# mLSTM heads by row groups and column groups, four modulation tiles in each head, and one modulation part computed beside the first dense product

## The chip, the cores and the metric

The kernel runs on 1 core of a Trainium2 chip. The metric is the device time of one execution in microseconds (us), the median over runs. Everything is float32; the large products are made from float32r halves (high and low parts), the small ones directly in float32.

## The reference

One layer of a decoder trunk on 256 prompt tokens and 8 sample sequences of 4 tokens (288 columns in all, N). Cut to what the change touches:

```python
mod = silu(c) @ w_ada + b_ada            # 9 rows; w_ada is 2048 x 12288
sh_a, sc_a, g_a, sh_c, sc_c, g_c = split(mod, 6)
h = rmsnorm(x, g) * (1 + sc_a) + sh_a
z = h @ w_in                             # the first dense product
# mLSTM, for each of 4 heads, state C (128 x 256) and n (128) per sequence
S    = (q @ k.T) * exp(logD - m)
num  = S @ v + w_inter * (q @ C)         # q @ C: the past state
den  = sum(S) + w_inter * (q @ n)
h    = num / max(abs(den), exp(-m))
C_new = dC * C + (ws * k).T @ v          # the update, one for each sequence
n_new = dC * n + sum(ws * k)
h    = h * rsqrt(mean(h * h) + eps)      # then gain and sigmoid(o)
x = x + g_a * (concat(rwkv, mlstm) @ w_out)
```

## The kernel before

The program is written out by hand for each engine, with semaphores; nothing is scheduled by a planner. Its stages in order of time:

* Modulation, parts 0 and 1. A part is 2048 columns of `w_ada` and comes as 16 tiles of 1 MiB through a ring of four SBUF slots (`ring`), loaded by SyncE's queue in program order. One `ada_step` on TensorE is one tile: 16 matmuls with 32 columns of weights and 128 moving columns, four of them side by side in the four column groups of the array. Four steps fill one bank; ScalarE copies it out (`ada_take`), and after a whole part `ada_turn` turns it and ScalarE stores it (`ada_store`).
* The first dense product, 50 tiles of `w_in` through the same ring. For each tile ScalarE makes the high half (`hi`), GpSimd the low half (`lo`), and TensorE runs 48 matmuls of 288 columns (`dense`). In the first 8 tiles ScalarE also feeds a convolution on VectorE and waits for it within each tile; then 8 tiles of v, 8 of o, and 26 of the RWKV part.
* Broadcasts and transposes for the mLSTM, then its 4 heads, then the RWKV-7 stage, then `w_out`, `w_q` and 256 PEER tiles, which take the time from about 945 us on.
* The 96 tiles of modulation parts 2 to 7 are handled between about 457 us and 900 us, as filling: `ada_more(count)` stands at fixed places in TensorE's stream, and takes the next `count` steps from one list, in order.

One mLSTM head h on TensorE before: after `s_ready` (VectorE's masked scores) three products into banks 1 to 3, in which the past state enters by 16 matmuls of 4 moving columns with a fresh 128x128 weight each; then nine updates (8 sequences and the prompt) one after the other in banks 4 and 5, each waiting until VectorE has used the bank two before; the scores of the next head; the sum of squares; and 7 modulation steps spread between. VectorE makes the denominator (`rec`), `hh`, the decays of the next head, and takes each update with two instructions: the state (128x256) and the normaliser (128x1). The state of each head is loaded and stored by GpSimd's queue (1 MiB each way).

Of the kernel before, what the change touches and what calls it, by code (L numbers as in the profile page):

```python
# [30 lines left out]
P = 128  # L31
# [21 lines left out]
def columns(sizes):  # L53
# [11 lines left out]
    ("seye", SM), ("sincl", SM), ("seq", NB), ("wreset", N), ("breset", N), ("mreset", N), ("sel", BH * P), ("fold", 4 * NS), ("seqcol", NB * SM), ("comp", 38)])  # L65
# [44 lines left out]
def constants():  # L110
# [50 lines left out]
    put(c1, CST1, "fold", fold)  # L161
    put(c1, CST1, "seqcol", np.broadcast_to(np.repeat(np.eye(NB), TS, axis=1), (P, NB, SM)))
# [16 lines left out]
def build(nc, T):  # L179
    ctx = ExitStack()  # L180
    with ctx:
# [45 lines left out]
        adas = words(M_ADAS, D)  # L227
        ymix = words(M_YMIX, KT, N)
# [38 lines left out]
        ktok_s = words(q6 + 2 * BH * P, BH, P, rows=SM)  # L267
        q7 = q6 + 3 * BH * P
        vtok = words(q7, 2, BH, DV + 1)
        vtok_s = words(q7 + 2 * BH * (DV + 1), BH, DV + 1, rows=SM)  # L270
# [6 lines left out]
        kwm = words(q4, NB, P, rows=SM)  # L277
        assert NB * P <= 4 * (ZXW + 1)
# [123 lines left out]
        wg_hi, wg_lo = parts("wg_hi", za, KT, 36), parts("wg_lo", za + KT * 36, KT, 36)  # L402
# [14 lines left out]
        n_wo = n_ada1 + 6 * ADA_TILES  # L417
# [74 lines left out]
        def ada_tile(j, quarter):  # L492

            return (n_ada0 + j * KT if j < 2 else n_ada1 + (j - 2) * KT) + 4 * quarter
# [8 lines left out]
        def parts_turned(j):  # L503

            return j + 4 if j else 1

# [6 lines left out]
        def _(sp):  # L513
# [27 lines left out]

            for j in range(2):
                ada(j)
            tiles(n_z, T["w_in"], 24, AT)
            tiles(n_z + 24, T["w_in"], 24)
            for j in range(2):
                load(n_z + 48 + j, T["w_in"][24 + j])
            for j in range(2, 8):
                ada(j)
# [149 lines left out]
        def _(pe):  # L699
# [14 lines left out]
            def ada_turn(j):  # L714

                pe.wait_ge(S("ada_copied"), 4 * (j + 1))
                if j > 2:
                    pe.wait_ge(S("mods_raw"), parts_turned(j - 1))
# [4 lines left out]
            def ada_step(j, quarter, q):  # L723
# [4 lines left out]
                if q == 0 and j > 2 and quarter == 1:  # L728
                    pe.wait_ge(S("mods_raw"), parts_turned(j - 1))
# [9 lines left out]
                if quarter == 0 and j > 0 and j != 2 and q == 3:  # L739
                    ada_turn(j - 1)  # L740
# [5 lines left out]
            pending = [(j, quarter, q) for j in range(2, 8) for quarter in range(4) for q in range(4)]  # L746
# [7 lines left out]
            def dense(n, hi, lo, i, bank, split=None):  # L754

                w_hi, w_lo = hi_slot(n), ring_lo[:, n % RING_SLOTS]
                for kt in range(KT):
                    if kt % 8 == 0:
                        pe.wait_ge(S("lo_ready"), i * 8 + (2 * dense_index(n) + kt // 8 + 1))
# [20 lines left out]
            pe.wait_ge(S("cond_ready"), 1)  # L780
# [34 lines left out]
            with pe.Fori(0, 6) as i:  # L815
                for j in range(4):
                    pe.wait_ge(S("z_free"), i * 4 + (24 + j + 1))
                    dense(n_z + 24 + j, h_hi, h_lo, i, j % 2, "h")
# [17 lines left out]
            for q, name in enumerate(("g", "ws")):  # L836
                for b in range(3):
                    w = P if b < 2 else SM
                    at = 4 * (2 * b + q)
                    mm = turn(ps[1][0:w, at:at + 4], row[name][:, b * P:b * P + w])  # L840
# [5 lines left out]
            for u, (what, b, g) in enumerate(fills):  # L846
                if u >= 4:
                    pe.wait_ge(S("turn_done"), u - 3)
                w = P if b < 2 else SM
                for j in range(4):  # L850
                    src = bv[:, 4 * g + j, b * P:b * P + w] if what == "v" else qk[:, BH + j, b * P:b * P + w]
                    mm = turn(ps[u % 4][0:w, j * P:(j + 1) * P], src)
# [11 lines left out]
            scores(0)  # L864
            for h in range(BH):
                pe.wait_ge(S("s_ready"), h + 1)
                pe.wait_ge(S(f"c_landed{h % 2}"), 16 * (h // 2 + 1))
                if h:
                    pe.wait_ge(S("num_used"), h)
                for half in range(3):  # L870
                    def vt(b, rows=P):
                        if half == 2:
                            return ones[0:rows, :]
                        src = vtok[:, b, h] if b < 2 else vtok_s[:, h]
# [4 lines left out]
                    mm = matmul(out[:, TP:N], vt(2, SM), dd[0:SM, 1, TP + P:DW], True, False)  # L879
                    if half < 2:  # L880
                        for b in range(NB):
# [3 lines left out]
                    else:  # L885
                        mm = matmul(out[:, TP:N], ones, qw[:, 1, :], False, True)
                mm.then_inc(S("num_ready"), 1)

                pe.wait_ge(S("kwm_ready"), h + 1)
                if h:  # L890
                    pe.wait_ge(S("ms_root"), h)
                    pe.wait_ge(S("upd_used"), h * NS)
                for u in range(NS):
                    if u >= 2:
                        pe.wait_ge(S("upd_used"), h * NS + u - 1)
                    out = ps[4 + u % 2][:, 0:DV + 1]
                    if u < NB:
                        mm = matmul(out, kwm[:, u, :], vtok_s[:, h, :])
                    else:
                        matmul(out, ktok[:, 0, h, :], vtok[:, 0, h, :], True, False)  # L900
# [1556 lines left out]
```

## Time and profile before

| what | us |
|---|---|
| median of 3 runs | 2921.88 (2921.21 to 2929.64) |
| the profiled execution | 2921.68 |
| its span, first to last instruction | 2919.9 |
| PE busy, POOL busy, DVE busy, ACT busy | 2725.9, 1771.7, 1121.3, 951.9 |
| mean granted TensorE clock | 0.955 |

How it is read. The windows view gives for a stretch of time its length, then the busy time and the count of instructions (x) of PE, PEld (weight loads), DVE (VectorE), ACT (ScalarE) and POOL (GpSimd), the granted TensorE clock (1.00 is 2.4 GHz, 0.50 is 1.2 GHz), the mean busy share of the DMA engines, and GB/s. The timeline gives start, duration, engine, line, operation, output and inputs with shapes, the count merged into the row, and in brackets the idle time before it with what released it. One float32 matmul leaves two records, so a modulation step of 16 matmuls is 32 records. The waits view gives the total, the number of times and the longest one. DMA issues give a median time from issue to landing.

### The profile page before, as it was taken

Reading aid. Unit: us, or ns where it says so; the run is one execution under the profiler, and the core shown is the slowest. Engines: PE = TensorE matmul, PEld = TensorE weight load, DVE = VectorE, ACT = ScalarE, POOL = GpSimd, SP = SyncE. Lnnn points to the kernel's source line nnn. Section 1 sums busy time; section 2 is a strip of 40 time slices with the busy share of each in tenths; the row PEclk is TensorE's granted clock in tenths of the full one; section 3 lists DMA queues with packets and bytes.
Section 4 is the critical chain, followed back from the end, with each engine's and each line's share of the span. In section 5 each row is a group of like instructions: output and inputs, shape, how many; then the busy total and the mean of one; then the engine's idle time right before and its main releaser. Section 6 shows DMA issues by size and latency. Waiting matters only on the chain.

```text
span 2919.9 us, 62759 instructions
## 1 busy us (share of the span) xinstructions
PE 2725.9 (93%) x25899; PEld 2620.6 (90%) x25899; DVE 1121.3 (38%) x2241; ACT 951.9 (33%) x1353; POOL 1771.7 (61%) x745
## 2 busy tenths in 40 slices
PE   5789999979875989999999999999999999999997
PEld 3689997768763979899999999999999999999997
DVE  0450664464237120896477313200131101455134
ACT  1343432131112333444333333333333333332333
POOL 0267771003211677688655577777777777888775
PEclk9899997679986999999999999999999999999999
DMA  9744445888664434344455444555544555554442
GB/s 374 263 142 165 165 160 212 290 294 285 233 208 162 159 126 162 130 158 158 174 182 181 164 171 159 179 185 187 177 159 172 184 182 189 185 183 174 169 163 104
DMA packets 150467, 544.94 MB, mean 187 GB/s; under 512 B 8984, under 2 KB 18856, under 8 KB 121512
## 3 DMA queue, kind: packets, MB, share of 16 engines
q1 hardware_dynamic: 136672, 505.18, 49.0%
q10 hardware_dynamic: 11480, 20.44, 1.9%
q0 software_dynamic: 2160, 17.03, 1.5%
q8 instruction: 125, 2.05, 0.3%
q14 instruction: 30, 0.25, 0.0%
HBM read 518.77 MB, written 23.84 MB: 186 GB/s over the span
## 4 chain that ended last, share of the span: by engine, by line
issue 39%; POOL 35%; PE 21%; DVE 3%; ACT 1%; POOLq 1%; DMA 0%; DVEq 0%; ACTq 0%
POOL ring_lo L605 34%; PE bank L701 21%; PE bank L704 0%; DVE staged L2106 0%; DVE y_lo L1758 0%; DMA kept<-in_w_ada 0%; POOLq L604 0%; DVE staged L2059 0%; ACT hi_peer L1337 0%; POOLq L609 0%; DVE staged L2093 0%; POOL h_lo L675 0%; POOL staged L694 0%; DVE staged L2095 0%; POOL staged L683 0%
## 5 line engine op out<-in xcount | busy, mean ns | idle before, releaser
L605 POOL TENSOR_TENSOR ring_lo<-kept,hi_peer 128x1024 fp32r<-128x1024 f32 x576 | 1441.6, 2526 | 496.9 <-ACT hi_peer L1337 496.9
L1337 ACT ACTIVATE hi_peer<-kept 128x1024 fp32r<-128x1024 f32 x576 | 578.1, 1051 | 1134.0 <-PE bank L701 1133.9
L701 PE MATMUL bank<-h_hi,ring_lo 128*128 128x288 f32 x3104 | 914.0, 294 | 0.0
L701 PE MATMUL bank<-h_hi,hi_peer 128*128 128x288 f32 x2304 | 686.1, 298 | 18.1 <-DVE h_lo L2152 10.3
L701 PE MATMUL bank<-h_lo,hi_peer 128*128 128x288 f32 x2304 | 680.7, 295 | 0.0
L701 PE MATMUL bank<-act_hi,hi_peer 128*128 128x288 f32 x2048 | 604.8, 295 | 6.7 <-POOL ring_lo L605 3.6
L701 PE MATMUL bank<-act_hi,ring_lo 128*128 128x288 f32 x2048 | 604.5, 295 | 0.0
L701 PE MATMUL bank<-act_lo,hi_peer 128*128 128x288 f32 x2048 | 604.2, 295 | 0.0
L701 PEld LDWEIGHTS bank<-h_hi,ring_lo 128*128 128x128 f32 x3104 | 585.8, 189 | 0.0
L701 PEld LDWEIGHTS bank<-h_hi,hi_peer 128*128 128x128 f32 x2304 | 432.4, 188 | 21.4 <-issue 16.2
L701 PEld LDWEIGHTS bank<-h_lo,hi_peer 128*128 128x128 f32 x2304 | 433.3, 188 | 0.0
L701 PEld LDWEIGHTS bank<-act_hi,hi_peer 128*128 128x128 f32 x2048 | 384.8, 188 | 8.4 <-POOL ring_lo L605 8.4
L701 PE MATMUL bank<-staged 64*64 64x64 f32 (+10 forms) x5264 | 339.9, 267 | 52.6 <-issue 18.3
L701 PEld LDWEIGHTS bank<-act_hi,ring_lo 128*128 128x128 f32 x2048 | 385.1, 188 | 0.0
L701 PEld LDWEIGHTS bank<-act_lo,hi_peer 128*128 128x128 f32 x2048 | 384.9, 188 | 0.0
L701 PEld LDWEIGHTS bank<-staged 64*64 64x64 f32 (+5 forms) x5264 | 283.3, 153 | 102.4 <-issue 51.8
L605 POOL TENSOR_TENSOR ring_lo<-kept,hi_front 128x1024 fp32r<-128x1024 f32 x100 | 243.3, 2453 | 205.1 <-ACT hi_front L1337 205.1
L2273 DVE CAST act_hi<-staged 128x576 fp32r<-128x576 f32 (+1 forms) x128 | 84.9, 663 | 578.1 <-PE bank L701 578.1
L701 PE MATMUL bank<-h_hi,hi_front 128*128 128x288 f32 x800 | 236.4, 296 | 11.4 <-POOL ring_lo L605 11.4
L701 PE MATMUL bank<-h_lo,hi_front 128*128 128x288 f32 x800 | 236.7, 296 | 0.0
L701 PE MATMUL bank<-kept,staged 128*32 128x128 f32 x4144 | 176.9, 328 | 64.0 <-DMA kept<-in_w_ada 36.9
L701 PEld LDWEIGHTS bank<-kept,staged 128*32 128x32 f32 x4144 | 137.9, 132 | 98.4 <-DMA kept<-in_w_ada 44.5
(219 smaller groups left out, 2371.0 us busy)
## 6 DMA issues: line engine op xcount, KB each, us to landing
kept<-in_peer_u SPq DMA_DIRECT2D x128, 1024.0 KB, 4.7
kept<-in_peer_v SPq DMA_DIRECT2D x128, 1024.0 KB, 5.5
kept<-in_w_ada SPq DMA_DIRECT2D x96, 1024.0 KB, 8.6
kept<-in_w_in SPq DMA_DIRECT2D x50, 1024.0 KB, 4.7
kept<-in_w_adaf SPq DMA_DIRECT2D x32, 1024.0 KB, 5.6
kept<-in_w_out SPq DMA_DIRECT2D x16, 1024.0 KB, 4.8
kept<-in_w_q SPq DMA_DIRECT2D x16, 1024.0 KB, 4.7
gates_spill<-staged ACTq DMA_DIRECT2D x24, 576.0 KB, 3.0
```

What stands on the lines that cost most here:

```text
L605: pool.tensor_tensor(ring_lo[:, n % RING_SLOTS, cols], ring[n % RING_SLOTS][:, cols], hi_slot(n)[:, cols].bitcast(F32), ALU.subtract).then ...
L701: return pe.matmul(out, lhsT, rhs, start=start, stop=stop)
L1337: return act.activation(out, in_, ACT.Copy)
L2273: dve.tensor_copy(act_hi[:, n % 2], a).then_inc(S("acts_hi"), 1)
```

## The change

It has three parts.

1. In the heads, the updates of the 8 sequences are made by 32-row matmuls: the keys of the 4 sequences of a half are masked so that each 32-row group holds one sequence (`kwm`, now 2 x 128 columns over 128 partitions in place of 8 x 128 over 32), and four updates go to four banks in the four row groups. The past state is applied by `qwm` (the queries masked by sequence, 32 columns of weights) with the state as moving data, 256 columns, in the four column groups of bank 0; ScalarE copies that bank to `past`, and two small matmuls add it to banks 1 and 2. The normaliser's eight small instructions become three for all sequences, with one matmul of 8 columns. The order inside a head changes on all three engines.
2. Each head has four modulation steps in one run at its end (`ada_more(4)`), in place of seven spread out, and one more stands ahead of the first head.
3. Modulation part 2 (`G_A`, 16 tiles) is computed in the first 16 tiles of the dense product, from two SBUF buffers of its own (`early`), with loads put between those of `w_in` in SyncE's queue. The list for `ada_more` has 80 steps in place of 96.

```diff
-            pending = [(j, quarter, q) for j in range(2, 8) for quarter in range(4) for q in range(4)]
+            pending = [(j, quarter, q) for j in range(2 + EARLY_PARTS, 8) for quarter in range(4) for q in range(4)]
+
+            def early_step(i, q):
+                pe.wait_ge(S(f"early{q % 2}_landed"), i * 32 + 16 * (q // 2 + 1))
+                if q == 0:
+                    pe.wait_ge(S("ada_copied"), i + 8)
+                for k_ in range(4):
+                    for g in range(4):
+                        mm = matmul(ps[6][32 * g:32 * g + 32, 0:P], silc[:, 4 * q + k_, :],
+                                    early[q % 2][:, k_ * 512 + g * P:k_ * 512 + (g + 1) * P],
+                                    q == k_ == 0, q == k_ == 3)
+                mm.then_inc(S("early_used"), 1)
+
+            def early_turn(i):
+                pe.wait_ge(S("ada_copied"), i + 9)
+                matmul(ps[7][:, bass.ds(i * (4 * NS), 4 * NS)], early_row, cst1("fold")).then_inc(S("ada_turned"), 1)
...
-            with pe.Fori(0, 6) as i:
+            with pe.Fori(0, EARLY_BODIES) as i:
                 for j in range(4):
                     pe.wait_ge(S("z_free"), i * 4 + (j + 1))
-                    dense(n_z + j, h_hi, h_lo, i, j % 2, "h")
+                    dense(n_z + j, h_hi, h_lo, i, j % 2, "h", {0: 0, 2: 3}.get(j))
+                    if j < 2:
+                        early_step(i, j + 1)
+                early_turn(i)
...
+            def update(h, u, bank):
+                pe.wait_ge(S("upd_used"), h * NS + (u - 3 if u >= 4 else 0))
+                matmul(ps[bank][:, 0:DV], kwm[QUAD[u % 4], u // 4, :], vtok_s[QUAD[u % 4], h, 0:DV]).then_inc(S("upd_ready"), 1)
...
+                for b in range(NB):
+                    mm = matmul(ps[0][QUAD[b % 4], 0:DV], qwm[:, b, :], cring[:, h % 2, b, :], b < 4, b >= 4)
+                mm.then_inc(S("num_ready"), 1)
...
-                            mm = matmul(out[:, TP + b * TS:TP + (b + 1) * TS],
-                                        cring[:, h % 2, b, half * P:(half + 1) * P], qw[:, 0, b * TS:(b + 1) * TS],
-                                        False, b == NB - 1)
...
+                for half in range(2):
+                    mm = matmul(ps[1 + half][:, TP:N], past[:, half * P:(half + 1) * P], cst1("seye"), False, True)
...
+                for u in range(4):
+                    update(h, u, 4 + u)
+                pe.wait_ge(S("head_taken"), 2 * h + 2)
+                for i in range(2):
+                    mm = matmul(ps[3][:, 0:N], ones, hsq[:, i, :], i == 0, i == 1)
+                mm.then_inc(S("ms_ready"), 1)
+                for u in range(4, NB):
+                    update(h, u, u)
+                pe.wait_ge(S("upd_used"), h * NS + 5)
...
                 pe.wait_ge(S("upd_used"), h * NS + NS - 1)
-                ada_more(3)
+                ada_more(4)
```

What stands there on TensorE after the products of the first head, from its first update on (banks by number; `kept,staged 32x128` is a modulation step, 257 columns are a state and its normaliser). Before:

```order
L701 MATMUL bank4<-staged 128x257
L701 MATMUL bank5<-staged 128x257
L701 MATMUL bank7<-kept,staged 32x128 x32
L701 MATMUL bank4<-staged 128x257
L701 MATMUL bank5<-staged 128x257
L701 MATMUL bank4<-staged 128x257
L701 MATMUL bank7<-kept,staged 32x128 x16
L701 MATMUL bank5<-staged 128x257
L701 MATMUL bank4<-staged 128x257
L701 MATMUL bank5<-staged 128x257
L701 MATMUL bank4<-staged 128x257 x2
L701 MATMUL bank0<-staged 128x256
```

And of the change, from the last of the next head's scores on:

```order
L748 MATMUL bank0<-staged 32x32
L748 MATMUL bank4<-staged 128x256
L748 MATMUL bank5<-staged 128x256
L748 MATMUL bank6<-staged 128x256
L748 MATMUL bank7<-staged 128x256
L748 MATMUL bank3<-staged,kept 128x288 x2
L748 MATMUL bank4<-staged 128x256
L748 MATMUL bank5<-staged 128x256
L748 MATMUL bank6<-staged 128x256
L748 MATMUL bank7<-staged 128x256
L748 MATMUL bank4<-staged 128x257 x2
L748 MATMUL bank4<-staged 128x8
```

The updates stand in fours, the sum of squares (bank 3) between them, the next head's scores ahead of them, and no modulation step among them; behind the last row come 64 matmuls of modulation.

ScalarE at the end of the third and the start of the fourth tile in a body of the first dense loop (the convolution's sigmoid, then the high half of a coming tile). Before:

```order
L1337 ACTIVATE staged<-bank 128x256 [waits zq_free]
L1337 ACTIVATE staged<-bank 128x8x4
L1337 ISA
L1337 ACTIVATE staged<-staged 128x8x3
L1334 ACTIVATE staged<-staged 128x312 [waits conv_ready]
L1432 REGISTER_ALU
L1337 ACTIVATE hi_front_51<-kept 128x1024 [waits weights_used,slot1_landed]
```

And of the change:

```order
L1409 ACTIVATE staged<-staged 128x312 [waits conv_ready]
L1447 REGISTER_ALU
L1448 REGISTER_ALU [waits early_used]
L1412 ACTIVATE staged<-bank 128x128 [waits ada_turned]
L1515 REGISTER_ALU
L1412 ACTIVATE hi_front_51<-kept 128x1024 [waits weights_used,slot1_landed]
```

The copy of the modulation row (128x128) now stands between the sigmoid of one tile and the high half of the next; TensorE's `early_turn` at the end of the body waits for it.

## Rows read from the trace of the kernel before

**Rows 1.** Windows: first dense tiles, then the four heads.

```profile
135.00:200.00 65.00, 56.09 (x404) 54.45 (x402) 44.80 (x59) 27.54 (x52) 39.27 (x17) 0.97 0.38 132
488.30:522.40 34.10, 34.10 (x307) 26.46 (x307) 14.04 (x36) 3.46 (x7) 3.21 (x6) 0.60 0.45 149
522.40:555.00 32.60, 32.17 (x319) 24.51 (x315) 17.29 (x41) 5.01 (x9) 1.61 (x3) 0.69 0.89 322
555.00:587.40 32.40, 32.40 (x309) 25.00 (x306) 14.01 (x36) 4.67 (x7) 1.07 (x2) 0.63 0.78 276
587.40:620.00 32.60, 26.22 (x311) 20.27 (x311) 18.60 (x33) 1.74 (x4) 1.61 (x3) 0.79 0.89 317
```

**Rows 2.** Waits in the heads, 488 to 620 us.

```profile
DVE staged L1920 <- PE bank L701: 37.7, 4, 12.1
```

**Rows 3.** Timeline of PE in the second head.

```profile
522.38 6.43 PE L701 MATMUL bank<-staged 128*128 128x256 f32 x44
...
533.36 3.64 PE L701 MATMUL bank<-kept,staged 128*32 128x128 f32 x64
536.93 3.14 PE L701 MATMUL bank<-staged 32*128 32x257 f32 x6
...
541.87 6.62 PE L701 MATMUL bank<-staged 32*128 32x257 f32 x15
```

**Rows 4.** Timeline of PE in the RWKV stage: a modulation step at full clock.

```profile
663.22 1.08 PE L701 MATMUL bank<-kept,staged 128*32 128x128 f32 x32
664.23 1.98 PE L701 MATMUL bank<-staged 64*64 64x128 f32 x64
```

**Rows 5.** Timeline of DVE in the second head.

```profile
531.46 0.46 DVE L1920 SCALAR_TENSOR_TENSOR staged<-bank,staged 128x288 f32<-128x288 f32 x1 [7.40 <-PE bank L701]
...
535.17 0.68 DVE L1744 TENSOR_SCALAR staged<-staged 128x256 f32<-128x256 f32 x3
535.77 0.17 DVE L1899 TENSOR_TENSOR staged<-staged 128x32 f32<-128x32 f32 x1
...
536.09 0.48 DVE L1936 SCALAR_TENSOR_TENSOR staged<-staged,bank 128x256 f32<-128x256 f32 x1
536.48 0.21 DVE L1937 SCALAR_TENSOR_TENSOR staged<-staged,bank 128x1 f32<-128x1 f32 x1
...
548.60 0.27 DVE L1907 TENSOR_TENSOR staged<-staged 128x128 f32<-128x128 f32 x1
...
549.68 0.17 DVE L1912 TENSOR_TENSOR staged<-bank,staged 32x32 f32<-32x32 f32 x1
551.25 1.95 DVE L1947 RECIPROCAL staged<-staged 128x288 f32<-128x288 f32 x1 [1.40 <-ACT staged L1340]
```

**Rows 6.** Timeline of PE from the last head to the RWKV stage.

```profile
610.89 1.96 PE L701 MATMUL bank<-kept,staged 128*32 128x128 f32 x64
613.46 1.08 PE L701 MATMUL bank<-kept,staged 128*32 128x128 f32 x32 [0.62 <-DMA kept<-in_w_ada]
619.76 1.94 PE L701 MATMUL bank<-kept,staged 128*32 128x128 f32 x32 [5.22 <-DMA kept<-in_w_ada]
...
627.30 1.24 PE L701 MATMUL bank<-staged 64*128 64x288 f32 x8
```

**Rows 7.** DMA issues between 457 and 682 us.

```profile
kept<-in_w_ada SPq DMA_DIRECT2D x51, 1024.0 KB, 7.7
```

**Rows 8.** Waits from 115 to 457 us, the first dense product.

```profile
PE bank L701 <- POOL ring_lo L605: 11.4, 8, 2.7
```

**Rows 9.** Timeline of ACT: high halves of two convolution tiles, then of two later ones.

```profile
148.41 2.00 ACT L1337 ACTIVATE hi_front<-kept 128x1024 fp32r<-128x1024 f32 x2
...
156.24 1.99 ACT L1337 ACTIVATE hi_front<-kept 128x1024 fp32r<-128x1024 f32 x2
...
207.23 2.02 ACT L1337 ACTIVATE hi_front<-kept 128x1024 fp32r<-128x1024 f32 x2 [5.81 <-PE bank L701]
...
213.41 2.01 ACT L1337 ACTIVATE hi_front<-kept 128x1024 fp32r<-128x1024 f32 x2 [3.88 <-PE bank L701]
```

**Rows 10.** Timeline of PE at the start of the first head.

```profile
488.27 9.43 PE L701 MATMUL bank<-staged 128*128 128x256 f32 x44 [2.25 <-DVE staged L1912]
```

**Rows 11.** Timeline of PE late in the sample states.

```profile
878.48 2.83 PE L701 MATMUL bank<-kept,staged 128*32 128x128 f32 x96
```

More of the change, by code:

```diff
@@ L401, in build @@
         assert q5 + D + KT * N <= za
-        wg_hi, wg_lo = parts("wg_hi", za, KT, 36), parts("wg_lo", za + KT * 36, KT, 36)
+        early = [words(q5 + D + KT * N + b * D, D) for b in range(2)]
+        assert (q5 + D + KT * N) % 8 == 0 and q5 + D + KT * N + 2 * D <= za + MT * N
+        wg_at = za + MT * N
+        wg_hi, wg_lo = parts("wg_hi", wg_at, KT, 36), parts("wg_lo", wg_at + KT * 36, KT, 36)
         y_hi, y_lo = parts("y_hi", m_yhi, KT, N), parts("y_lo", M_YMIX, KT, N)
@@ L836, in _ @@
             for q, name in enumerate(("g", "ws")):
-                for b in range(3):
-                    w = P if b < 2 else SM
+                for b in range(2):
                     at = 4 * (2 * b + q)
-                    mm = turn(ps[1][0:w, at:at + 4], row[name][:, b * P:b * P + w])
+                    turn(ps[1][:, at:at + 4], row[name][:, b * P:(b + 1) * P])
+                for g in range(4):
+                    mm = matmul(ps[1][QUAD[g], 4 * (4 + q):4 * (4 + q) + 4], row[name][:, TP:N], ident[0:BH, 0:BH])
             mm.then_inc(S("cols_ready"), 1)
@@ L848, in _ @@
                     pe.wait_ge(S("turn_done"), u - 3)
[L849 removed]
                 for j in range(4):
[L851 to L852 removed]
+                    src = bv[:, 4 * g + j] if what == "v" else qk[:, BH + j]
+                    if b < 2:
+                        mm = turn(ps[u % 4][:, j * P:(j + 1) * P], src[:, b * P:(b + 1) * P])
+                        continue
+                    for c in range(4):
+                        mm = matmul(ps[u % 4][QUAD[c], j * P:(j + 1) * P], src[:, TP:N], ident)
                 mm.then_inc(S("turn_ready"), 1)
@@ L887, in _ @@
-                mm.then_inc(S("num_ready"), 1)
[L889 to L900, printed above, removed]
-                        mm = matmul(out, ktok[:, 1, h, :], vtok[:, 1, h, :], False, True)
-                    mm.then_inc(S("upd_ready"), 1)
-                    if u in (1, 4):
-                        ada_more(2 if u == 1 else 1)
+                    matmul(out[:, TP:N], vt(2, SM), dd[0:SM, 1, TP + P:DW], True, False)
@@ L909, in _ @@
+                out = ps[4][:, 0:DV + 1]
+                matmul(out, ktok[:, 0, h, :], vtok[:, 0, h, :], True, False)
+                matmul(out, ktok[:, 1, h, :], vtok[:, 1, h, :], False, True)
+                matmul(ps[4][:, DV + 1:DV + 1 + NB], ktok_s[0:SM, h, :], cst1("seq", rows=SM)).then_inc(S("upd_ready"), 1)
                 pe.wait_ge(S("upd_used"), h * NS + NS - 1)
-                for i in range(2):
-                    mm = matmul(ps[5][:, 0:N], ones, hsq[:, i, :], i == 0, i == 1)
```

204 lines of the change are left out of this document (128 added, 76 removed).

## Prediction

> **What bounds the kernel now.** I read the windows first, because the page's 93% for TensorE is a mean over stages with different limits and the change touches two of them. In the four heads TensorE is busy for nearly the whole stretch, VectorE for about half of it, and the granted clock is 0.60 to 0.79, so TensorE runs mostly at the lower of its two levels [rows 1]. The head starts stand at 488.3, 522.4, 555.0 and 587.4 us, a pitch of 99.1 / 3 = 33.0 us. The waits then say who is kept waiting: VectorE waits for TensorE at the start of its denominator, 37.7 us in four heads [rows 2], and the timeline shows TensorE going from one block to the next, updates, modulation steps and products [rows 3]. So a head is bound by the length of TensorE's stream, at a low clock. The last head is followed by a stretch in which TensorE waits for modulation tiles, 0.62 and 5.22 us [rows 6]. The first dense product is another matter. In its first 8 tiles ScalarE sets the pace: its high halves come every 156.24 - 148.41 = 7.83 us, and TensorE waits for the low halves behind them 8 times, 11.4 us in all [rows 8, 9]. Later they come at 213.41 - 207.23 = 6.18 us, which is TensorE's own pace, and whatever is added to TensorE there lengthens the stage. The PEER tiles are not touched.
>
> **Part 3, the early tiles.** Added: 16 steps and 4 turns. A step between other work at full clock takes 664.23 - 663.22 = 1.01 us [rows 4], so 16.2 us, and four one-matmul turns about 0.25 us each (a quarter of a step), 1.0: 17.2 us. What can hide it is the idle 11.4 us of the first 8 tiles, so the floor is 17.2 - 11.4 = 5.8. But the first two turns do not hide. The row copy that a turn waits for stands on ScalarE behind the third tile's sigmoid, one whole ScalarE cycle late. In that region tile j+2 starts about 3.5 us after ScalarE takes tile j (1.0 us of a high half, 2.4 us of a low half), so a fourth tile ends about 1.9 us after ScalarE takes the third, and the copy comes at 7.8: TensorE stands for about 6 us less the 3 to 4 us of steps that have already pushed it back. Followed tile by tile, with ScalarE's cycle unchanged, tile 11 of the dense product and its turn end 6.8 us later than now, and the second 8 steps and two turns, of which 4 steps and one turn are still to come, add 4.3: 11.1 us. I take 12 for a little lower clock behind those two waits (it is 0.97 there now [rows 1]). The bounds are 5.8 and, if nothing hides and both waits add 3 us, 23. ScalarE's copy, 0.3 us twice within its chain, is in it. The loads: 16 MiB more beside the first 16 tiles, 132 GB/s now and about twice that, well under the 322 GB/s of the second head [rows 1]; each early load is asked for one and a half tiles ahead, 9 us against 7.7 in a much busier stretch [rows 7]. I cost them at nothing; if landing took 12 us, each step would stand 3 us.
>
> **Ahead of the first head.** TensorE now waits 2.25 us for the scores there [rows 10]. The eighth modulation step is new, and ScalarE must copy it before it makes the decays' exponentials, which it did not have to do. Scores (1.6), step (1.8 at half clock) and copy (0.3) go in line where the exponential was free at once; part is returned by the smaller key mask. +2.5 us (0 to 4).
>
> **The head's period.** I price TensorE's blocks at both clocks. At half clock a step is 3.64 / 2 = 1.82 us [rows 3] for four rounds of four matmuls with 128 columns, 0.46 a round, so a round of 256 columns 0.91; at full clock 0.5. Full-array matmuls, by 15 records with about 1,700 columns in 6.62 us [rows 3], 3.9 ns a column, half of it at full clock. No row shows four 32-row matmuls of 256 columns side by side. I take the column-group round for them (0.91); one after the other they would be 4 x 1.05, by 6.3 us for six records (three updates) in 3.14 us [rows 3], 3.3 us more for each four, half of it behind VectorE.
>
> From a head's start, half clock (full clock in brackets): past state 1.8, first product 1.8, denominator's product ready at 3.6 (1.9); two more products and the past's two matmuls, 7.0 (3.6). VectorE: the denominator to `hh` takes 535.17 - 531.46 = 3.7 us, of which the last 0.75 needs all products [rows 5]: 7.8 (5.6). Query masks, 0.3 and one 128x256 product of 0.5, then the next head's scores, 549.85 - 548.60 = 1.25 [rows 5]: 9.9 (7.7). Eight updates at the pitch 536.48 - 536.09 = 0.39 [rows 5], without the eight small ones. TensorE meanwhile does the next scores, the first four updates at 9.5 (4.9), and the sum of squares at 11.8 (7.4), after ScalarE's square; the second four at 12.7 (7.9). VectorE ends them at 14.3 (10.8), TensorE the prompt's update at 15.1 (10.8). Four steps, 7.3 (4.0): the next head starts at 22.4 (14.8). VectorE's end of the head, reciprocal onward, lies beside the four steps, and its next decays are done before they are wanted.
>
> Which clock? The four heads show 0.60, 0.69, 0.63 and 0.79 [rows 1], mean 0.68, a half-clock share of 0.64. The period is 0.64 x 22.4 + 0.36 x 14.8 = 19.7 us, and three of them save 99.1 - 59.1 = 40.0 us.
>
> The new head leaves TensorE more idle than the old one, with waits of a microsecond or two between its blocks. On this the Trainium skill, in "TensorE: Matmul & The Clock Gate", the section on oscillation, says that the array is throttled unless activity releases it and that repeated waits between bursts keep it cold. By that rule the heads would stay at half clock, 22.4 us each, which is 8 us more than I take; the heads now are near fully busy and yet at 0.60 to 0.79, so the trace shows already that busy time alone does not give the high clock.
>
> **The last head to the RWKV stage.** Now 627.3 - 587.4 = 39.9 us [rows 1, 6]. Six steps stand behind the last update, and the last tiles come late. After, the update ends 13.6 us into the head (0.64 x 15.1 + 0.36 x 10.8); seven steps follow, four on tiles that landed long before, three each about 7.7 us behind a freed slot [rows 7] but overlapped: 16 us for all of it, by the 16 to 18 us of the same stretch now. 30 us: saves 10 (bounds 4 and 14).
>
> **Behind it.** 80 steps run out 5 places earlier. Three of these stood where TensorE then waits anyway, two in a block of three that takes 2.83 us [rows 11]: -1 us.
>
> **Sum.** +12 + 2.5 - 40 - 10 - 1 = -36.5 us against the profiled execution's 2921.7 (0.2 under the median, no difference): 2885.
>
> **The rivals.**
> * *Full clock.* Less work in small 4-column matmuls, and four groups filled at once, hold the clock up: three periods of 14.8 save 14.7 more, 2870. Against it: the waits in each head. 12%.
> * *Half clock throughout*, the rule above: 3 x 22.4, 2893. 16%. The trace of before, half clock for two thirds of the heads, speaks for it.
> * *Late tiles.* A head moves 4 tiles, a state in and a state out, 6.3 MB; at the 317 to 322 GB/s of two heads now that is 20 us, no less than the period forecast. If the four steps in a run stand for slots, the period goes to 25: 2901. Against it: all four slots have had most of a period to fill. 9%.
> * *Slower.* The same with the state's traffic in front of the tiles in each head: at 180 GB/s the period is 35, and then 3 x 2 - 10 + 12 + 2.5 - 1 gives 2931. It turns slower from a period of 31.8 us, 198 GB/s; the second and fourth head moved over 315 [rows 1]. 3%.
> * *The groups do not run side by side.* 3.3 us more for each four, half hidden: about 3 us a head, 2897; small beside the rest, and within the range. 5%.
>
> **How the numbers follow.** The forecast has 55%, with its own range 2872 to 2898 (period 17 to 22, dense part 6 to 18). The range that leaves out 2 in 10 takes in the half-clock and serial cases and most of the full-clock one: 2866 to 2903. A change of 0.3%, 8.8 us, is about what can be told from none; only the slower rival and the tail of the late tiles reach 2913: faster 95%, same 2%, slower 3%.
>
> **What would show it.** The dense product ends 10 to 14 us later, at about 469, with two waits of TensorE of 3 to 4 us at the fourth and eighth tile for ScalarE's copy. Head starts stand 17 to 22 us apart, VectorE's wait at its denominator falls from 9 us a head to under 4, DMA runs near 320 GB/s there, and the RWKV stage starts about 35 us earlier than 627. I am wrong if the period is over 25 (look for TensorE waiting for `w_ada` tiles or for VectorE's updates) or if the dense product grows by 17 or more.

## The result and the profile after

The changed kernel takes 2900.81 us (median of 8 runs, 2896.16 to 2903.28), the kernel before, beside it, 2923.61 (8 runs, 2909.67 to 2929.64): a ratio of 0.9924, with an interval of 0.9906 to 0.9942. It is 22.8 us faster where 36.5 were forecast, and the time lies inside the range. In the profiled executions the span went from 2919.9 to 2899.8 us, 20.1 less.

The page of the profile after, its busy times and the slices of TensorE's clock:

```profile
span 2899.8 us, 62885 instructions
PE 2687.4 (93%) x25957; PEld 2587.4 (89%) x25957; DVE 1112.4 (38%) x2220; ACT 954.1 (33%) x1357; POOL 1771.5 (61%) x745
PEclk9899998879986999999999999999999999999999
```

The page says little: TensorE still has 93%. The windows of the changed kernel say more. The first row answers to the first of [rows 1]; then come the stretch ahead of the heads, the four heads, and the end of the fourth with the start of the RWKV stage. The columns are those of [rows 1]: length, busy time of PE, PEld, DVE, ACT and POOL, granted clock, share of the DMA engines, GB/s.

```profile
135.00:200.00 65.00, 58.46 (x559) 55.51 (x561) 40.21 (x52) 26.64 (x53) 38.35 (x16) 0.95 0.67 242
473.80:511.50 37.70, 30.51 (x432) 22.62 (x432) 13.08 (x29) 8.29 (x19) 1.31 (x2) 0.73 0.83 289
511.50:531.90 20.40, 19.84 (x204) 14.71 (x208) 12.83 (x32) 3.37 (x6) 2.53 (x5) 0.67 0.16 45
531.90:554.30 22.40, 16.22 (x208) 11.86 (x200) 15.44 (x38) 5.05 (x8) 2.29 (x5) 0.90 1.03 402
554.30:571.60 17.30, 16.80 (x215) 12.46 (x207) 12.75 (x30) 5.06 (x8) 1.10 (x3) 0.93 0.72 258
571.60:590.00 18.40, 13.53 (x198) 9.98 (x197) 14.14 (x24) 2.30 (x6) 1.62 (x3) 1.00 0.97 352
590.00:611.00 21.00, 14.73 (x134) 10.54 (x135) 8.36 (x10) 8.16 (x18) 0.00 (x0) 0.59 0.89 333
```

A head is 20.4, 22.4 and 17.3 us long instead of 34.1, 32.6 and 32.4, and the clock is up in three of the four. The second head is the longest although its clock is 0.90: TensorE is busy for 16.2 us of it only. The DMA engines carry 45 GB/s in the first head and 402 in the second.

The waits of the heads, 511 to 600 us (engine, line, what it waited for: us in total, times, longest), answer to [rows 2]:

```profile
DVE staged L2016 <- PE bank L748: 15.7, 4, 9.0
PE bank L748 <- DMA kept<-in_w_ada: 14.1, 6, 5.7
```

VectorE's wait at the denominator fell from 37.7 us to 15.7. New is the second row: TensorE stands for modulation tiles. PE's timeline shows where, and how long the groups take (answers to [rows 3], [rows 6] and [rows 10]):

```profile
511.46 1.23 PE L748 MATMUL bank<-staged 128*32 128x256 f32 x16 [3.67 <-DVE staged L2005]
515.20 8.18 PE L748 MATMUL bank<-staged 128*128 128x256 f32 x30
...
525.52 0.87 PE L748 MATMUL bank<-staged 32*128 32x256 f32 x8
...
528.34 3.70 PE L748 MATMUL bank<-kept,staged 128*32 128x128 f32 x128
531.86 1.05 PE L748 MATMUL bank<-staged 128*32 128x256 f32 x16
...
547.40 1.08 PE L748 MATMUL bank<-kept,staged 128*32 128x128 f32 x32 [1.49 <-DMA kept<-in_w_ada]
552.63 1.94 PE L748 MATMUL bank<-kept,staged 128*32 128x128 f32 x32 [4.15 <-DMA kept<-in_w_ada]
554.34 1.93 PE L748 MATMUL bank<-staged 128*32 128x256 f32 x16
...
592.81 1.94 PE L748 MATMUL bank<-kept,staged 128*32 128x128 f32 x32 [5.70 <-DMA kept<-in_w_ada]
...
601.01 2.29 PE L748 MATMUL bank<-staged 64*128 64x288 f32 x8
```

The head starts are the lines with x16. The one of the second head (531.86) finds its four steps in one block of 3.70 us just before it; the third (554.34) comes behind two waits for tiles, 5.64 us. The RWKV stage starts at 601.01 instead of 627.30.

The first dense product: PE's waits for the early row copy, and then, in ACT's timeline, the high halves that begin one body of four tiles and the next.

```profile
159.02 0.41 PE L748 MATMUL bank<-staged 128*128 128x36 f32 x2 [2.98 <-ACT staged L1412]
194.51 0.41 PE L748 MATMUL bank<-staged 128*128 128x36 f32 x2 [2.96 <-ACT staged L1412]
```

```profile
226.95 2.01 ACT L1412 ACTIVATE hi_front<-kept 128x1024 fp32r<-128x1024 f32 x2 [3.70 <-PE bank L748]
257.19 2.01 ACT L1412 ACTIVATE hi_front<-kept 128x1024 fp32r<-128x1024 f32 x2 [3.70 <-PE bank L748]
```

A body of four tiles takes 257.19 - 226.95 = 30.24 us. Before, the high halves come 6.18 and 6.43 us apart by turns, and the fourth behind the one at 213.41 [rows 9] stands at 238.64, so four tiles took 25.2 us:

```profile
238.64 2.01 ACT L1337 ACTIVATE hi_front<-kept 128x1024 fp32r<-128x1024 f32 x2 [3.87 <-PE bank L701]
```

Each edge of the stages, in us of the profiled executions ("dense ends" is ScalarE's first copy behind the last product, the others are by PE's timeline; "heads" is from the first head's start to the RWKV stage's, "stage" from there to the first matmul of `w_out`; the experiments below are read at the same places):

| kernel | dense ends | first head | RWKV starts | `w_out` | heads | stage |
|---|---|---|---|---|---|---|
| before | 455.30 | 488.27 | 627.30 | 944.58 | 139.0 | 317.3 |
| changed | 474.06 | 511.46 | 601.01 | 923.03 | 89.6 | 322.0 |

So the dense product costs 18.8, the way to the first head 4.4 more, the heads give back 49.5, the RWKV stage takes 4.7, and 1.5 are left for the rest.

### The profile page after: what moved, and what is told of

It reads as the page before. It is cut to its first block, busy times and chain, and to the rows that moved or that the text cites. A ratio compares the mean times of both kernels' runs of the same rounds, so it can differ in the third digit from the quotient of the medians.

```text
span 2899.8 us, 62885 instructions
## 1 busy us (share of the span) xinstructions
PE 2687.4 (93%) x25957; PEld 2587.4 (89%) x25957; DVE 1112.4 (38%) x2220; ACT 954.1 (33%) x1357; POOL 1771.5 (61%) x745
## 4 chain that ended last, share of the span: by engine, by line
issue 40%; POOL 35%; PE 19%; DVE 3%; DMA 2%; ACT 1%; POOLq 1%; SPq 0%; DVEq 0%; ACTq 0%
POOL ring_lo L652 35%; PE bank L748 18%; DMA kept<-in_w_ada 2%; PE bank L751 0%; DVE staged L2203 0%; DVE y_lo L1845 0%; POOLq L651 0%; DVE staged L2156 0%; ACT hi_peer L1412 0%; POOLq L656 0%; DVE staged L2190 0%; POOL staged L741 0%; POOL h_lo L722 0%; POOL staged L730 0%; DVE staged L2192 0%
## 5 line engine op out<-in xcount | busy, mean ns | idle before, releaser
L748 PE MATMUL bank<-staged 64*64 64x64 f32 (+11 forms) x5736 | 324.0, 269 | 75.6 <-issue 28.4
L748 PEld LDWEIGHTS bank<-staged 64*64 64x64 f32 (+7 forms) x5736 | 270.7, 146 | 122.8 <-issue 71.3
L748 PE MATMUL bank<-kept,staged 128*32 128x128 f32 x3744 | 153.9, 316 | 66.8 <-DMA kept<-in_w_ada 46.8
L1412 ACT ACTIVATE staged<-bank 128x384 f32<-128x384 f32 (+7 forms) x285 | 108.9, 417 | 309.7 <-PE bank L748 284.5
```

Of the source, the lines that this page charges most:

```text
L748: return pe.matmul(out, lhsT, rhs, start=start, stop=stop)
L1412: return act.activation(out, in_, ACT.Copy)
```

## The experiments

**Part 3 alone.** The kernel before with only the third part of the change, modulation part 2 beside the dense product (16 steps fewer later), heads untouched.

> The kernel before with part 3 alone: early tiles in the first 16 dense tiles, old heads with seven steps each, 80 steps in the list. Theory (part 3 is a cost that the heads pay back only if they get shorter; filling removed from the end of the list is worth nothing): dense product +16 to 17 us as in the changed kernel, heads unchanged at a pitch of 33, the list ends 16 places earlier, most of these places in stretches where TensorE waits anyway: total +5 to +12 us against before. Rival (moving 16 steps out of the middle saves each of them once, 1.0 to 1.8 us): total within 3 us of before or under it.

2927.26 us against 2924.33 (ratio 1.0011, 1.0000 to 1.0022), 2.9 more where 5 to 12 were expected, and inside the rival's 3 us. The first head starts at 506.72, 18.5 later than before; the heads take 137.8, and the stage 307.7, 9.6 less. The early tiles alone bring nothing.

**Fewer steps, old heads.** The same, with four steps in each old head in place of seven:

```diff
-                    if u in (1, 4):
-                        ada_more(2 if u == 1 else 1)
+                    if u == 1:
+                        ada_more(1)
...
-                ada_more(3)
+                ada_more(2)
```

> The same, but the old heads have four steps each (one after the second update, one after the next scores, two at the end). Theory (old heads are bound by TensorE's stream, at 1.0 to 1.8 us a step): pitch of heads falls by 3 steps, about 4.5 us, to about 28.5, so the total is 14 to 20 us under the run with seven, while 12 steps go to later places and take 5 to 10 us of it back. Rival (the gain of the changed kernel's heads is mostly the packing of matmuls, the steps only filled waits): pitch stays over 31.

2924.84 us, ratio 1.0004 (0.9995 to 1.0014), 2.4 us under the run with seven steps where a net gain of 4 or more was expected. The heads take 125.2 instead of 139.0, and the stage takes back 9.6 (307.7 to 317.3) for the 12 steps moved into it. So of the 49.5 us that the changed heads save, about 13.9 are steps moved out, which are mostly paid later, and 125.2 - 89.6 = 35.6 come from the rest of the new head: the packed updates, the packed past states, the shorter normaliser and the new order. No run takes these apart.

**The copy earlier.** The changed kernel, with ScalarE's copy of the early row one place up, ahead of the sigmoid's wait:

```diff
-                    if j == 3:
-                        early_take(i, 0)
...
+                    if j == 2:
+                        early_take(i, 0)
```

(and the same for the second turn).

> The changed kernel with ScalarE's copy of the early row moved one place up, behind the high half in the third tile's turn instead of behind that tile's sigmoid. Theory (the two waits of 3.0 us for that copy, and the lower clock of 0.82 to 0.89 behind them, are what made the dense product 5 us dearer than the steps alone): both waits vanish, the dense product ends 7 to 10 us earlier, total 7 to 10 us less than the changed kernel. Rival (TensorE has slack there against ScalarE's pace of 7.8 us a tile, so that the wait only moves): the idle time comes back as waits for the low halves, total within 3 us.

2889.41 us, ratio 0.9886 (0.9870 to 0.9903), 11.4 below the changed kernel's median. The dense product ends at 465.98, 8.1 earlier, and the first head starts at 503.10, 8.4 earlier. Windows of this kernel, the stretch of the first row above:

```profile
135.00:200.00 65.00, 64.28 (x674) 61.28 (x673) 42.40 (x57) 27.73 (x54) 38.58 (x16) 1.00 0.79 279
```

TensorE is busy for 64.3 of 65 us at full clock, where it was 58.5 at 0.95. The two waits come to 5.9 us, and the last high half of the fourth body is 9.6 us earlier (247.58 instead of 257.19): the rest is mostly the clock behind them (below). Of the 9.6, 1.5 are lost again further on. Both kernels have the same wait of 2.03 us for a low half there (at 322.39 in the changed kernel, at 312.77 here), and behind it the clock stays up in the one and falls in the other (PE's timeline of this kernel, and windows of the changed one and of this one):

```profile
312.77 0.40 PE L748 MATMUL bank<-h_hi,hi_front 128*128 128x288 f32 x1 [2.03 <-POOL ring_lo L652]
```

```profile
322.30:328.30 6.00, 5.91 (x44) 5.91 (x45) 5.71 (x4) 1.33 (x4) 6.00 (x4) 1.00 0.37 153
312.70:318.70 6.00, 5.92 (x33) 5.93 (x34) 5.71 (x4) 1.32 (x4) 6.00 (x4) 0.72 0.36 153
```

**The exponential first.** ScalarE makes the first head's decays before it copies the eighth step:

```diff
-            ada_more(1)
             decays(0)
+            ada_more(1)
```

> The changed kernel with the first head's exponentials on ScalarE ahead of the copy of the eighth modulation step. Theory (the first head starts late because ScalarE waits for that step first): the scores are ready about 2.3 us earlier, first head starts that much earlier, total 2 to 3 us less. Rival (the first head waits for VectorE's key mask and the transposes): no change in the distance from the end of the dense product to the first head.

2893.24 us, ratio 0.9888 (0.9871 to 0.9905). PE's timeline of this kernel, the starts of the first and second head:

```profile
509.53 1.07 PE L748 MATMUL bank<-staged 128*32 128x256 f32 x16 [0.69 <-DVE staged L2005]
...
511.96 4.54 PE L748 MATMUL bank<-staged 128*128 128x256 f32 x30
...
524.92 1.05 PE L748 MATMUL bank<-staged 128*32 128x256 f32 x16
```

The wait is 0.69 us instead of 3.67. The head behind it takes 524.92 - 509.53 = 15.4 us instead of 20.4: its block of thirty 256-column rows takes 4.54 us where it took 8.18. The head starts 1.9 us earlier. The dense product ends 1.7 later here (475.72), for the clock fell behind the wait of 2.03 us in this run too; from its end to the first head it is 33.8 us instead of 37.4, so the move is worth 3.6. ACT's timeline shows what was in line, first of the changed kernel, then of this one:

```profile
507.88 0.28 ACT L1412 ACTIVATE staged<-bank 128x128 f32<-128x128 f32 x1 [16.69 <-PE bank L748]
508.18 1.28 ACT L1409 ACT_TABLE_LOAD   x1
...
492.87 1.28 ACT L1409 ACT_TABLE_LOAD   x1
```

Behind the copy of the step (507.88) ScalarE loads a table for 1.28 us before it can make the exponential; with the exponential first, this load stands 15 us earlier, in time in which ScalarE was idle. Not all of the gain arrives: the second head starts 6.9 us earlier, the RWKV stage 3.3. The third head runs behind a wait of 4.16 us for a tile, at a clock of 0.58; in the changed kernel, behind 4.15, it was 0.93:

```profile
547.38:564.70 17.32, 16.77 (x81) 11.23 (x70) 8.85 (x22) 5.05 (x8) 0.02 (x1) 0.58 0.60 229
```

**Both moves.**

> Both moves on ScalarE together: the early row's copy one place up, and the first head's exponentials ahead of the copy of the eighth step. Theory (the two are independent: no wait for the copy in the dense product, and a wait of 0.7 in place of 3.7 us ahead of the first head, so that its whole stream runs at the high clock, 15.4 us in place of 20.4): 8.4 + 1.9 + 5.0, about 15 us less than the changed kernel in the traces, 2881 to 2886 us. Rival (the first head's clock is chance, not the wait ahead of it): a first head of 20 us again, 2889 or more.

2881.55 us (2880.58 to 2887.12), ratio 0.9866 (0.9846 to 0.9885): 19.3 below the changed kernel (17 by the two ratios), and the fastest kernel here that computes everything. Its dense product ends at 466.31, the heads take 83.8 and the stage 320.6. The window of its first head, and the timeline of PE at the end of its second:

```profile
500.20:515.60 15.40, 14.90 (x202) 11.47 (x206) 12.65 (x32) 3.37 (x6) 2.49 (x5) 1.00 0.42 131
```

```profile
531.18 1.08 PE L748 MATMUL bank<-kept,staged 128*32 128x128 f32 x32 [1.41 <-DMA kept<-in_w_ada]
536.22 1.93 PE L748 MATMUL bank<-kept,staged 128*32 128x128 f32 x32 [3.96 <-DMA kept<-in_w_ada]
```

The first head runs at clock 1.00. The second (515.59 to 537.92, 22.3 us) still waits for its tiles, so ScalarE's order is not what makes it long.

**A quarter of each tile.** In the tiles of the modulation parts 3 to 7 only the first quarter is loaded, and all four rounds of a step read it; the modulation is therefore another one. All instructions stay, and 0.75 MiB of each tile is not moved.

```diff
+                        ks = 1 if j >= 2 + EARLY_PARTS else 4
-                        sp.dma_start(ring[n % RING_SLOTS].rearrange("p (k c) -> p k c", k=4),
-                                     src.rearrange("(k p) c -> p k c", p=P)).then_inc(landed[n % RING_SLOTS], 16)
+                        sp.dma_start(ring[n % RING_SLOTS].rearrange("p (k c) -> p k c", k=4)[:, 0:ks],
+                                     src.rearrange("(k p) c -> p k c", p=P)[:, 0:ks]).then_inc(landed[n % RING_SLOTS], 16)
...
+                    at = i * 512 if j < 2 + EARLY_PARTS else 0
```

> The changed kernel, but of each modulation tile of parts 3 to 7 only a quarter is loaded and all 16 matmuls read that quarter, so that the outputs are not the reference's; TensorE's work is the same. Theory (the waits for tiles in the second head, 5.6 us, and behind the last, 8.5 us, come from the tiles' traffic beside the states'): both vanish, second head's pitch falls from 22.5 to about 16 us, the RWKV stage starts 12 to 15 us earlier, total 12 to 16 us less. Rival (behind the waits stands something else that ends hardly earlier, the stores of the states or VectorE's products): under 6 us less.

2862.79 us, ratio 0.9793 (0.9770 to 0.9817). The heads take 77.6, 11.9 less, as expected, though the first one takes 21.2. That tiles come late because of the states' traffic is not shown by this: it shows that smaller tiles come in time. Not expected: the stage behind them takes 296.0 instead of 322.0. No wait for a tile stands in that stage in either kernel, so a second cost of the tiles was open.

**Eight steps in each head.** The changed heads without part 3: all 96 steps later, eight at the end of each head.

```diff
-                ada_more(4)
+                ada_more(8)
```

> Parts 1 and 2 without part 3: the new heads, 96 steps in the list, with eight steps at the end of each head in place of four. Theory (TensorE's stream sets the new heads' pitch, so four steps more cost 4 to 7 us a head, but the dense product has its old length): dense product 17 us shorter than in the changed kernel, heads 16 to 28 us longer with late tiles in each, 4 to 6 more steps at the end of the RWKV stage: total 0 to 12 us over the changed kernel. Rival (part 3 costs more than it saves, as it does alone): total under the changed kernel.

2946.47 us, ratio 1.0086 (1.0069 to 1.0104), slower than before, and 45.7 over the changed kernel where 0 to 12 were expected. Heads 152.0. Waits of this kernel from 488 to 680 us:

```profile
PE bank L703 <- DMA kept<-in_w_ada: 44.2, 19, 7.3
```

The window of its first two heads:

```profile
494.20:534.60 40.40, 27.48 (x332) 20.34 (x336) 14.55 (x36) 3.65 (x7) 3.22 (x6) 0.64 0.59 218
```

A run of eight steps on a ring of four slots has four tiles that are asked for only when the run has begun: TensorE waits 19 times, and the clock falls as well. This kernel doesn't tell what part 3 is worth, since it is the length of the run that failed. The next one does.

**Four steps in each head, part 3 undone.** The same with four (the edit is against the run with eight), and the 16 steps that are then over in the RWKV stage and behind it: one more at each of its twelve levels, the rest at the last places, which stood empty:

```diff
-                ada_more(8)
+                ada_more(4)
...
-                    ada_more(1)
+                    ada_more(2)
```

> The changed heads (row groups, column groups, four steps in each) with the eighth modulation part undone from the dense product: all 96 steps are back, four at the end of each head, and the 16 that would be left over go one each into the levels and behind the past products of the RWKV stage. Theory (the early tiles of the dense product cost 18.8 us and buy only about 10 us later): the first head starts at about 494 instead of 511.5, the four heads take about 90 us as in the changed kernel, RWKV begins near 584, and its stage is 9 to 12 us longer than the 322 of the changed kernel; about 2894, 6 to 8 us below the changed kernel. Rival (the 16 steps are as dear later as early, because they wait for tiles there): 1.2 us or more each, no gain, 2900 to 2905.

2903.69 us (2900.59 to 2906.80), ratio 0.9927 (0.9910 to 0.9943). That is the changed kernel's time, 2.9 more by the medians, which these runs don't tell apart. The first head starts at 494.69, 16.8 earlier than in the changed kernel; the heads take 88.4; but the stage takes 343.6 instead of 322.0, 1.35 us for each of the 16 steps, where 9 to 12 us were expected. The rival was right. As it was written, the change has its gain from the heads: part 3 took its steps from places that cost 22 us to one that costs 17, a difference that the medians don't show. What they cost late depends on the places, though: part 3 alone, above, took 16 steps out of the same stage, which became only 9.6 us shorter.

**Which tiles make the RWKV stage long.** The quarter loads again, once for the 27 steps ahead of the RWKV stage only and once for the 53 behind.

> The changed kernel, with a quarter of a tile loaded for the 27 steps that lie before the RWKV stage, whose matmuls read that quarter four times; the tiles of the later 53 steps are whole again. Theory (tile traffic beside the RWKV stage is what makes TensorE stand there, so the 26 us that the run with all tiles quartered won behind the heads need the later tiles): RWKV begins at 588 to 591, its stage stays at 318 to 323 us, about 2888. Rival (the stage is shorter because it starts at another clock phase or with a filled ring): its stage is near 296, about 2862.

> The opposite half: whole tiles for the 27 steps before the RWKV stage, a quarter of a tile for the 53 later ones. Theory (traffic beside the RWKV stage): heads as in the changed kernel, RWKV begins at 598 to 601 (the four tiles of the ring there are already quarters), and its stage takes about 296 to 300 us instead of 322; about 2875. Rival (start of the stage decides): 322 us, about 2900.

Heads only: 2885.51 us, ratio 0.9871 (0.9854 to 0.9887); heads 70.2, stage 317.6. Later only: 2877.22 us, ratio 0.9834 (0.9816 to 0.9852); heads 89.1, stage 295.1. The 27 us are in the traffic beside that stage. The heads' 70.2 flatters: the profiled execution of that kernel is the fastest of its four, 10.8 us under their median, and its first head ran at full clock behind the same wait as ever (timeline and window of that kernel):

```profile
509.99 1.07 PE L749 MATMUL bank<-staged 128*32 128x256 f32 x16 [3.66 <-DVE staged L2007]
...
512.42 4.53 PE L749 MATMUL bank<-staged 128*128 128x256 f32 x30
```

```profile
509.99:525.38 15.39, 14.89 (x200) 11.46 (x204) 12.64 (x32) 3.38 (x6) 2.48 (x5) 1.00 0.08 15
```

The kernel with all tiles quartered is the same up to there and has the same wait of 3.66 us, and its first head took 21.2 us at a clock of 0.64. So a wait of this length does not settle the clock behind it.

For the stage, first the changed kernel, then the one with later quarters, in the same stretch (windows):

```profile
660.00:780.00 120.00, 104.33 (x2982) 93.55 (x2974) 37.36 (x52) 20.07 (x40) 32.12 (x14) 0.96 0.71 230
```

```profile
660.00:780.00 120.00, 118.73 (x3520) 107.47 (x3514) 42.83 (x60) 26.00 (x53) 32.84 (x15) 1.00 0.24 69
```

With 69 GB/s beside it TensorE is busy for 118.7 us of 120 and has 3,520 matmul records; with 230 GB/s it is busy for 104.3 and has 2,982. The waits of the whole stage name the idle time as "issue", which is time in which the engine waited for nothing that the profile shows. The changed kernel, then the one with later quarters:

```profile
PE bank L748 <- issue: 32.4, 23, 3.7
```

```profile
PE bank L749 <- issue: 13.9, 10, 4.0
```

18.5 us of the 26.9 are these gaps, 23 against 10 of about the same length. The page lists transfers on two queues of kind "instruction", 0.8 MB in this stage, and gives their share of the same DMA engines. The trace has each of their packets with its start and length. On the larger queue 47 packets of 16 KiB land in the 322 us of this stage, and 22 of the 23 gaps end 1.2 to 1.6 us after one of them has landed; so do 9 of the 10 in the kernel with later quarters, and 16 of 17 in the kernel before. So by all that the times show, TensorE stands for its instructions in these gaps. That they come late because tiles stand before them would fit the quarter loads, and is argued: a packet takes 1.0 us in the median in all three, and what it waits for before it starts the trace doesn't show.

## Why the prediction was right, and where its terms were off

**What bounded the kernel.** Right: the heads were bound by TensorE's stream, and shortening it shortened them, from 139.0 us to 89.6, with VectorE's wait down from 37.7 to 15.7.

**Part 3 in the dense product, forecast 12, measured 18.8.** The mechanism was right: two waits of 3 to 4 us for ScalarE's copy were forecast, and there are two, of 2.98 and 2.96 us. The size was off, by the clock behind the waits and by the price of a step. I wrote "I take 12 for a little lower clock behind those two waits". The clock halves behind each of them, while TensorE is fully busy again (windows of the changed kernel, two right behind the first wait, one behind the second):

```profile
161.00:163.00 2.00, 2.00 (x10) 2.00 (x10) 1.62 (x3) 0.24 (x3) 2.00 (x2) 0.50 0.00 0
163.00:165.00 2.00, 2.00 (x25) 1.83 (x28) 2.00 (x1) 0.00 (x0) 1.69 (x1) 0.73 0.00 0
...
196.50:198.50 2.00, 2.00 (x12) 2.00 (x11) 1.63 (x3) 0.23 (x3) 2.00 (x2) 0.57 0.00 0
```

PE's timeline has the pitch of the dense matmuls there:

```profile
160.35 0.29 PE L748 MATMUL bank<-h_lo,hi_front 128*128 128x288 f32 x1
160.48 0.29 PE L748 MATMUL bank<-h_hi,ring_lo 128*128 128x288 f32 x1
...
161.27 0.44 PE L748 MATMUL bank<-h_hi,hi_front 128*128 128x288 f32 x1
161.51 0.44 PE L748 MATMUL bank<-h_lo,hi_front 128*128 128x288 f32 x1
```

They start 0.13 us apart at first and 0.24 apart from 160.8 to 163.9 us, which loses 1.4 us, and it is nearly the same behind the second wait. With these, taking the waits away gives 5.9 + 2 x 1.4 = 8.7 of the 9.6 us that it gave at the end of the fourth body. The other term is a step between dense tiles. The prediction read 6.18 us as TensorE's pace for a tile, but it is one of two that alternate, 6.3 in the mean; so a step costs (30.24 - 25.2) / 4 = 1.25 us with its share of the turn, where 17.2 / 16 = 1.08 was counted, 2.8 us over 16 steps. The two together are 5.6 of the 7.7 between the 11.1 that I had counted and 18.8. Another 1.0 lies ahead of the tiles: the first product waits to 122.38 us instead of 121.40. The last 1.1 is open. The bound of 17 for "wrong" was passed by 1.8 us, so by its own sign this term was wrong.

**Ahead of the first head, forecast 2.5 (0 to 4), measured 4.4.** The copy before the exponential was the cause, as the run with the exponential first shows: it gave 3.6 of it back, from the end of the dense product. The term left out is ScalarE's table load of 1.28 us between the copy and the exponential, which the sum of scores, step and copy doesn't have. What I didn't see either is the clock of the head behind the wait: 20.4 us with it, 15.4 in both runs with a short one, but 15.4 too in one run with the long one.

**The heads, forecast 50 with the tail, measured 49.5.** Three periods are 60.1 us where 59.1 were forecast, and the tail is 29.4 us after 30. The sum is right, and its makeup is not. A head at full clock takes 15.4 us (14.8 forecast, the run with both moves), the first one at a mean clock of 0.67 takes 20.4 (22.4 forecast for half clock throughout). I took the clock of the old heads, 0.68, as a mean; the new ones show 0.67, 0.90, 0.93 and 1.00, nearer the rival of full clock, which would have been worth 14.7 us more. The rival of late tiles took much of it back: 1.49 + 4.15 us in the second head, and 14.1 - 5.6 = 8.5 in the tail, where 5.8 stood before [rows 6]. Both rivals held in part, in different heads, and nearly cancelled. With quarter tiles, which take most of that away, the heads come to 77.6 us, and to 70.2 in the trace whose first head had the full clock.

**DMA near 320 GB/s in the heads.** Wrong: 45, 402, 258 and 352. The four steps stand at the end of a head and the ring is full until they run, so nothing is asked for in the first head and everything at once in the second, with a state out and a state in. That is how the program stands, and the rates fit it. I had argued against late tiles that "all four slots have had most of a period to fill"; they had, but beside the states: from the first head's steps at 528.34 to the wait at 547.40 is 19 us.

**The groups side by side.** Right, and now seen. Four updates (x8, since a float32 matmul leaves two records) take 0.87 us in the first head, in the middle of which the clock goes up (0.78 in the mean), and 0.71 in the fourth at full clock; one update alone took 0.70 at full clock before (the changed kernel, then before):

```profile
580.27 0.71 PE L748 MATMUL bank<-staged 32*128 32x256 f32 x8
...
603.99 0.70 PE L701 MATMUL bank<-staged 32*128 32x257 f32 x2 [0.27 <-DVE staged L1937]
```

The rival of serial groups is out.

**Slower.** It did not come: tiles came 5.6 us late in one head and 8.5 in the tail. The run with eight steps a head shows how near it lay: the same heads with a run longer than the ring take 152.0 us.

**Behind the heads, forecast -1, measured +4.7.** Wrong, and the largest miss beside the dense product. I counted the steps that fall out and took the rest of the stage as fixed. It isn't: its "issue" gaps are 32.4 us in 23 pieces, and were 27.0 in 17 before, a difference of 5.4. That they follow the traffic is shown by the quarter loads; but the kernel before had more traffic there, 227 GB/s against 208, and fewer of them. Why this kernel has six more is open.

**The rule on waits and the clock.** The Trainium skill, "TensorE: Matmul & The Clock Gate", in its section on oscillation, describes a kernel that waits for a DMA between short bursts, so that every burst starts cold. The forecast stretched it to the heads, whose waits are shorter than the work between them; there it would have given half clock throughout. Half clock throughout did not come, with 0.90 to 1.00 in three heads; their waits of 0.2 to 1.1 us left the clock up. The clock fell where I didn't look for it: behind the 3-us waits in the dense product, to 0.50 in all seven kernels that have them, and behind the 3.7 us ahead of the first head, in six of the seven kernels that have it. Behind the wait of 2.03 us in the dense product it fell in four kernels of twelve. A wait makes the fall possible, and its length alone doesn't tell whether it comes.

## What to carry to other kernels

A wait of 3 us on TensorE can cost more than its length, since what follows may run at half clock for a while: two waits of 5.9 us in all cost 9.6, and a first head 5.0. Price it with a range, since the same wait in the same stream may also cost nothing more, as one run shows. Look for the last instruction on the other engine that it hangs on, and move that up first; look too for a table load that the move brings in line or takes out of it. Two such moves gave 19.3 us here, nearly as much as the change itself (22.8). Small pieces placed "where there is room" are only free until the transfers that they need have to come: don't put more of them in a run than the ring has slots, and price a moved step at both places, 17 us early against 22 us late in this case. When the sum comes out right, read the parts: here a gain in clock and a loss in late tiles cancelled, and only the parts showed that both could still be had.

## What was not expected of the hardware

* After a wait of 2.98 us the granted clock stayed at 1.00 for 1.7 us of work, was 0.50 for 3.2 us with TensorE fully busy, and rose again. Behind the 3.67 us ahead of the first head it was 0.50 from 514 to 524 us. It was 1.00 in the whole of the same head behind waits of 0.69 and 0.45 us, and once behind 3.66 us.
* Four matmuls of 256 columns on four row groups take about the time of one: 0.71 us at full clock, where one of 257 columns took 0.70.
* Transfers that nobody waits for slow TensorE in a stage of many small matmuls: 295.1 us at a quarter of the modulation tiles' bytes, 322.0 with whole tiles, with not one wait for a tile. In the heads alone, quartered tiles left that stage at 317.6. Nearly all of TensorE's gaps there end just after a packet of instructions has landed.
